# A decoder trunk on one core: both norms' sides by tiles of 128 tokens, and five weight slots with the low part over the raw weights

## The reference, cut to what matters

```python
for l in range(2):
    x = layer_norm(ALPHA * x + 0.5 * swiglu(x, ffn1_w_gate[l], ffn1_w_up[l], ffn1_w_down[l]), ...)
    x = layer_norm(ALPHA * x + hybrid_mixer(x, ...), ...)
    x = layer_norm(ALPHA * x + 0.5 * swiglu(x, ffn2_w_gate[l], ffn2_w_up[l], ffn2_w_down[l]), ...)

def swiglu(x, w_gate, w_up, w_down):              # inner width 2816
    return (silu(x @ w_gate) * (x @ w_up)) @ w_down
```

## Time and profile before

| | |
|---|---|
| median of 3 runs | 1401.45 us (1401.25 to 1403.24) |
| the profiled execution | 1403.12 us, its span 1400.8 us |
| PE busy | 97% of the span |
| DVE, ACT, POOL busy | 66%, 47%, 5% |
| mean granted clock of PE | 0.992 |
| HBM read | 232 MB, 167 GB/s over the span |

### The profile page before, as it was taken

One profiled execution on the slowest core, in us unless ns is written; L12 is line 12 of the kernel. 1 busy time (PEld: TensorE's weight loads), 2 busy tenths in 40 slices (PEclk: granted clock), 3 DMA queues, 4 the chain that ended last, 5 costly groups with the idle time before them and its releaser, 6 DMA issues.

```text
span 1400.8 us, 20707 instructions
## 1 busy us (share of the span) xinstructions
PE 1353.8 (97%) x8440; PEld 1203.2 (86%) x8440; DVE 928.8 (66%) x978; ACT 663.4 (47%) x674; POOL 69.9 (5%) x59
## 2 busy tenths in 40 slices
PE   7999989999999999999999999899999999999997
PEld 6888879899899978888878888798998999788886
DVE  5665666788885656565665666676988656666565
ACT  5444455574354354444454444555744543544442
POOL 2980000000000000000000000000000000000000
PEclk9999999999999999999999999999999999999999
DMA  8655644544355545655545565436434555365562
GB/s 275 227 180 180 192 151 133 164 136 123 121 154 185 174 150 183 195 191 180 172 158 180 185 195 190 143 122 185 121 99 142 178 184 173 110 227 180 180 191 79
DMA packets 182312, 234.19 MB, mean 167 GB/s; under 512 B 5808, under 2 KB 161072, under 8 KB 182128
## 3 DMA queue, kind: packets, MB, share of 16 engines
q1 hardware_dynamic: 182016, 231.68, 52.1%
q0 software_dynamic: 240, 1.71, 0.4%
HBM read 232.33 MB, written 1.05 MB: 167 GB/s over the span
## 4 chain that ended last, share of the span: by engine, by line
PE 95%; DVE 3%; ACT 2%; issue 0%; DMA 0%; SPq 0%; DVEq 0%; ACTq 0%
PE ps L1283 24%; PE ps L1294 21%; PE ps L1223 11%; PE ps L1224 11%; PE ps L1225 11%; PE ps L1282 10%; PE ps L1286 1%; DVE wlo L748 1%; PE ps L1243 1%; PE ps L1392 1%; DVE z L864 1%; ACT whi L463 1%; PE ps L1410 0%; PE ps L1430 0%; PE ps L1440 0%; PE ps L1435 0%
## 5 line engine op out<-in xcount | busy, mean ns | idle before, releaser
L748 DVE TENSOR_TENSOR wlo<-raw,whi 128x2048 fp32r<-128x2048 f32 (+2 forms) x221 | 497.6, 2253 | 188.6 <-ACT whi L463 188.5
L463 ACT ACTIVATE whi<-raw 128x2048 fp32r<-128x2048 f32 (+2 forms) x221 | 415.3, 1881 | 354.2 <-PE ps L1225 206.2
L1283 PE MATMUL ps<-xpair,whi 128*128 128x512 f32 x1408 | 489.5, 397 | 5.0 <-DVE xpair L805 5.0
L1282 PE MATMUL ps<-xpair,wlo 128*128 128x256 f32 x1232 | 345.5, 280 | 0.0
L1283 PEld LDWEIGHTS ps<-xpair,whi 128*128 128x128 f32 x1408 | 255.2, 188 | 54.5 <-DVE xpair L805 5.7
L1223 PE MATMUL ps<-xpair,whi 128*128 128x256 f32 (+2 forms) x896 | 259.7, 290 | 10.7 <-DVE xpair L805 5.4
L1224 PE MATMUL ps<-xpair,whi 128*128 128x256 f32 (+2 forms) x896 | 255.9, 286 | 0.0
L1225 PE MATMUL ps<-xpair,wlo 128*128 128x256 f32 (+2 forms) x896 | 255.8, 286 | 0.0
L1282 PEld LDWEIGHTS ps<-xpair,wlo 128*128 128x128 f32 x1232 | 233.1, 189 | 8.1
L1223 PEld LDWEIGHTS ps<-xpair,whi 128*128 128x128 f32 (+2 forms) x896 | 170.4, 190 | 13.4 <-issue 12.4
L1224 PEld LDWEIGHTS ps<-xpair,whi 128*128 128x128 f32 (+2 forms) x896 | 170.3, 190 | 2.0 <-issue 1.0
(11 more groups left out here) (221 smaller groups left out, 1680.2 us busy)
## 6 DMA issues: line engine op xcount, KB each, us to landing
raw<-w_in SPq DMA_DIRECT2D x60, 1024.0 KB, 5.2
raw<-ffn_w_up SPq DMA_DIRECT2D x44, 1024.0 KB, 5.3
raw<-ffn_w_down SPq DMA_DIRECT2D x44, 1024.0 KB, 4.9
raw<-ffn_w_gate SPq DMA_DIRECT2D x43, 1024.0 KB, 5.4
raw<-w_br SPq DMA_DIRECT2D x12, 1024.0 KB, 5.0
raw<-w_out SPq DMA_DIRECT2D x8, 1024.0 KB, 4.9
raw<-mla_w_uq SPq DMA_DIRECT2D x4, 576.0 KB, 3.9
raw<-mla_w_ukv SPq DMA_DIRECT2D x2, 1024.0 KB, 5.6
```

What stands on the lines that cost most here:

```text
L463: act.activation(whi[:, k % RING, 0:n], raw[:, k % RING, 0:n], ACT.Copy).then_inc(w_hi, 1)
L748: dve.tensor_tensor(wlo[:, k % RING, 0:n], raw[:, k % RING, 0:n], whi[:, k % RING, 0:n].bitcast(F32), ALU.subtract).then_inc(w_lo, 1)
L1282: pe.matmul(ps[:, bank + c, 0:SEQ], wl[:, kk, cols], xhi[:, kk, :], start=False, stop=False)
L1283: last = pe.matmul(ps[:, bank + c, :], wh[:, kk, cols], xpair[:, kk, :, :], start=kk == 0, stop=kk == KC - 1)
```

## The change

Tokens cross every norm in two tiles of 128. In the last two units of a stage (`last_rows`) PE does banks 0 and 1 of both, then the rest; the transposes of tile 0 stand between products of bank 2. DVE and ACT share a tile's rows (lower 512 features on DVE, upper on ACT), and DVE orders its work tile by tile. The next stage begins with work that a single tile allows: in an FFN the gate and up unit of step 0 are done with the tokens as stationary operand (`tile_gate`, `tile_up`), and the product is transposed (`tile_split`); in a mixer mv comes first, by halves of the depth with 512 columns. `RING` is five, `wlo` lies over `raw`, `load` waits for `w_used` of the unit five before, and `hi` waits for the load alone; `hi` and `lo` of the next stage's first units stand in the last FFN step. The loops over the FFN's steps are written out. The last up unit is done in three terms without a sum on ACT and DVE. On ACT the silu of `ml_qk` goes behind the copies of `k_nope`; the gate units use banks 5 and 6 and the branches 7 and 4. `g_row` and `b_row` lie in another region.

```diff
-RING = 3
+RING = 5
-    raw = sb("raw", [P, RING, UNIT])
-    whi, wlo = sb("whi", [P, RING, UNIT], F32R), sb("wlo", [P, RING, UNIT], F32R)
+    r_raw = region(4 * RING * UNIT)
+    raw, wlo = place("raw", [P, RING, UNIT], F32, r_raw), place("wlo", [P, RING, UNIT], F32R, r_raw)
+    whi = sb("whi", [P, RING, UNIT], F32R)
...
+    BANK |= {"mv0": 6, "mv1": 7}
+    GATE_BANK, BRANCH_BANK = (5, 6), (7, 4)
+    FFN_GATE, FFN_UP, TILE_BANK = 6, 4, (6, 4)
...
-            sp.wait_ge(w_lo, free_no(l, k, f))
+            if n >= RING:
+                sp.wait_ge(w_used, done_no(n - RING))
...
+                load_x(1)
...
     @block.scalar
-            act.wait_ge(w_loaded[k % RING], loaded_no(l, k, f))
-            act.wait_ge(w_used, free_no(l, k, f))
+            act.wait_ge(w_loaded[n % RING], (n // RING + 1) * 16)
...
+            if nth:
+                hi(base + 2)
+            tile_silu(0)
+            hi(base + 3)
+            tile_silu(1)
+            hi(base + 4)
+            for j in range(1, NF):
+                hi(base + 3 * j + 2)
+                gate_of(j)
+                silu_of(j)
+                if base + 3 * j + 3 < N_UNITS:
+                    hi(base + 3 * j + 3)
+                if j < NF - 1:
+                    up_of(j)
+                if base + 3 * j + 4 < N_UNITS:
+                    hi(base + 3 * j + 4)
...
+        def layer_norm(l, w):
+            turn = l * 3 + w
             act.activation(warm[:, :], C("eps", 1), ACT.Sqrt)
+            for t in range(TT):
+                act.wait_ge(ln_var, tile_no(turn, t))
+                act.activation(std[:, t:t + 1], mv[:, t, 1:2], ACT.Sqrt,
                                bias=C("eps", 1, 1)).then_inc(ln_std, 1)
...
+                act.wait_ge(ln_shift, tile_no(turn, t))
+                act.activation(z[:, t, 512:], ps[:, 2 * t + 1, :], ACT.Identity, bias=shift[:, t:t + 1],
+                               scale=rstd[:, t:t + 1]).then_inc(rows_up, 1)
+                scale_x(turn + 1, t)
...
-            hi(l, m0 + 11)
-            act.wait_ge(conv_tap, l * 32 + 16)
-            act.activation(ml_qk[:, 0:4, :], ml_qk[:, 0:4, :], ACT.Silu).then_inc(qk_silu, 1)
+            hi(m0 + 13)
             act.wait_ge(k_done, l + 1)
             copy(flat(k_nope[:, 0:2, :]), "kn0").then_inc(k_copied, 1)
             copy(flat(k_nope[:, 2:4, :]), "kn1").then_inc(k_copied, 1)
...
+            hi(m0 + 14)
+            act.wait_ge(conv_tap, l * 32 + 16)
+            act.activation(ml_qk[:, 0:4, :], ml_qk[:, 0:4, :], ACT.Silu).then_inc(qk_silu, 1)
...
+        scale_x(0, 0)
         act.wait_ge(half_loaded, 16)
         act.activation(whi[:, 0, 0:UNIT // 2], raw[:, 0, 0:UNIT // 2], ACT.Copy).then_inc(half_hi, 1)
         act.wait_ge(w_loaded[0], 16)
         act.activation(whi[:, 0, UNIT // 2:], raw[:, 0, UNIT // 2:], ACT.Copy).then_inc(w_hi, 1)
+        scale_x(0, 1)
+        hi(1)
+        hi(2)
...
     @block.vector
+            for j in range(1, NF):
+                lo(base + 3 * j + 2)
+                if j == 1:
+                    tile_split()
+                gate_sum(j)
+                if base + 3 * j + 3 < N_UNITS:
+                    lo(base + 3 * j + 3)
+                product(j)
+                split(j)
+                if base + 3 * j + 4 < N_UNITS:
+                    lo(base + 3 * j + 4)
...
+        def scale_x(stage, t):
+            dve.wait_ge(rows_turned, half_no(stage, t, 0))
...
+                for k in range(4):
+                    last = dve.tensor_scalar(xf[:, k, tok], ps[:, 4, k * P:(k + 1) * P], par_col(l, "ln_g", 8 * w + k),
+                                             par_col(l, "ln_b", 8 * w + k), ALU.mult, ALU.add)
+            last.then_inc(x_lower, 1)
+            dve.wait_ge(x_lower, tile_no(stage, t))
+            split_x(stage, t, 0)
...
             measure(0)
             measure(1)
             aggregate(0)
-            measure(2)
             invert(0)
             if last_turn:
                 store_rows(0)
+                measure(2)
                 measure(3)
...
+            normalise(0)
+            scale_x(turn + 1, 0)
+            measure(2)
+            dve.wait_ge(x_upper, tile_no(turn + 1, 0))
+            split_x(turn + 1, 0, 1)
             measure(3)
             aggregate(1)
             invert(1)
...
+            normalise(1)
+            scale_x(turn + 1, 1)
+            dve.wait_ge(x_upper, tile_no(turn + 1, 1))
+            split_x(turn + 1, 1, 1)
...
     @block.tensor
+        def last_rows(n, pick, stage):
+            for bank in range(4):
+                for kk in range(2):
+                    if bank == 2 and kk == 0:
+                        tile_rows(n - 1, 1, pick[0]).then_inc(w_used, 1)
+                    last = tokens(n, bank, kk, *pick[1](kk, bank // 2), False, True)
+                    if kk == 1 and bank < 3:
+                        last.then_inc(y_bank, 1)
+                    if bank == 2 and kk == 0 and stage < 3 * DEPTH:
+                        turn_rows(stage, 0)
+            last.then_inc(w_used, 1)
...
+            tile_gate(0)
+            turn_rows(stage, 1)
+            if stage:
+                tile_up(0)
+            tile_gate(1)
+            if stage == 0:
+                tile_up(0)
+            tile_up(1)
...
+                if j == 1:
+                    pe.wait_ge(tok_hid, tile_no(nth, 1))
+                    for c in range(2):
+                        for t in range(TT):
+                            last = pe.transpose(ps[:, FFN_UP + 1, c * SEQ + t * P:c * SEQ + (t + 1) * P],
+                                                hid[:, t * SEQ + c * P:t * SEQ + (c + 1) * P], ident)
+                    last.then_inc(hid_turned, 1)
+                    paired(FFN_UP, up)
+                    pe.wait_ge(hid_lo, step_no(l, w, 0))
+                    paired(FFN_UP + 1, up).then_inc(w_used, 1)
...
+            first_values(0, 0)
+            turn_rows(stage, 1)
+            first_values(0, 1)
+            first_values(1, 0).then_inc(w_used, 1)
+            first_values(1, 1).then_inc(w_used, 1)
+
+            project(2, "c0")
...
-            pe.wait_ge(k_copied, l * 2 + 2)
-            half_tokens(10, ("mv0", "mv1"), 0)
-            half_tokens(11, ("mv0", "mv1"), 256)
...
                         if b == h == 0:
-                            pe.wait_ge(rg_ready, l * 2 + 2)
-                        two_chunks(4 + i, k).then_inc(w_used, 1)
+                            pe.wait_ge(mo_ready, l * 2 + i + 1)
+                        two_chunks(GATE_BANK[i], k).then_inc(w_used, 1)
```

More of the change, by code:

```diff
@@ L39 @@
 MIX_BASE = U_FFN
[L40 removed]
+N_UNITS = DEPTH * U_LAYER
 C_MQ, C_MV, C_GATES, C_MO = 704, 1728, 2240, 2248
@@ new lines, in scale_x @@
+        def scale_x(stage, t):
+            act.wait_ge(rows_turned, half_no(stage, t, 1))
+            tok = slice(t * P, (t + 1) * P)
+            for k in range(4, KC):
+                src = ps[:, 5, (k - 4) * P:(k - 3) * P]
+                if stage == 0:
+                    last = act.activation(xf[:, k, tok], src, ACT.Copy)
+                else:
+                    l, w = (stage - 1) // 3, (stage - 1) % 3
+                    last = act.activation(xf[:, k, tok], src, ACT.Identity, bias=par_col(l, "ln_b", 8 * w + k),
+                                          scale=par_col(l, "ln_g", 8 * w + k))
+            last.then_inc(x_upper, 1)
@@ L808, in layer_norm @@
-        def layer_norm(l, w, early):
+            if nth:
+                lo(base + 2)
+            tile_product(0)
+            lo(base + 3)
+            tile_product(1)
+            lo(base + 4)
+            for j in range(1, NF):
+                lo(base + 3 * j + 2)
[8 more added lines that the diff above has]
+                    lo(base + 3 * j + 4)
@@ new lines, in split_x, with scale_x @@
+        def split_x(stage, t, half):
+            part, tok = slice(4 * half, 4 * half + 4), slice(t * P, (t + 1) * P)
+            dve.tensor_copy(xhi[:, part, tok], xf[:, part, tok]).then_inc(x_hi, 1)
+            dve.wait_ge(x_hi, half_no(stage, t, half))
+            dve.tensor_tensor(xlo[:, part, tok], xf[:, part, tok], xhi[:, part, tok].bitcast(F32),
+                              ALU.subtract).then_inc(x_ready, 1)
+        def scale_x(stage, t):
+            dve.wait_ge(rows_turned, half_no(stage, t, 0))
+            tok = slice(t * P, (t + 1) * P)
+            if stage == 0:
+                last = dve.tensor_copy(xf[:, 0:4, tok], ps[:, 4, :].rearrange("p (k n) -> p k n", k=4))
+            else:
+                l, w = (stage - 1) // 3, (stage - 1) % 3
+                for k in range(4):
[4 more added lines that the diff above has]
+            split_x(stage, t, 0)
@@ new lines, in two_chunks, with tile_columns, paired @@
+                last = features(ps[:, bank, c * SEQ:(c + 1) * SEQ], n, width, slice(c * P, (c + 1) * P), xh, xl, n_k)
+            return last
+        def tile_columns(out, n, kk, x_kk, t, start, stop):
+            wh, wl = slot(n, out.shape[1])
```

(39 more changed lines are left out.)

798 lines of the change are left out of this document (380 added, 418 removed).

## The result

The changed kernel takes 1363.44 us (median; 1362.52 to 1364.15) against 1402.35 us of the kernel before on the same chip: ratio 0.9715, interval 0.9701 to 0.9728. The forecast was 1366.2 us with a range of 1359 to 1382. The profiled execution took 1363.81 us with a span of 1361.5, so 39.3 us of span went where 35.3 had been forecast.

A forecast was written before the change was run, and what follows sets the result against it. TensorE (PE), busy 97% of the 1400.8 us span, was taken to bound the kernel. The terms summed to -35.3 us, taking the 1401.45 us median to a forecast of 1366.2 us, range 1359 to 1382.

The forecast's parts named there:

- five crossings: At the five norm crossings, working tile by tile leaves 3.0 us lost in place of 27.2: -24.2 us.
- last wait of an FFN: At four FFN ends, the wait for the last unit's `lo` shrinks by 0.3 us each: -1.2 us.
- k_nope and rot_sw: In the mixers, PE's wait for k_nope goes and 0.6 us for rot_sw stays: -2.8 x 2 = -5.6 us.
- rg with its drop: In the mixers, gates on free banks end the rg wait and its clock drop: -4.2 x 2 = -8.4 us.
- products and switches: PE's work: mv and rv -1.4, tile products +1.9, transposes of hid +1.75, switches +2; sum +4.3 us.
- start: At the kernel's start, units 0 and 1 end at 29.2 us against 27.3: +1.9 us (0 to 3.5).
- Rival 1: At crossings, tile chains on DVE stay on the path and the clock drops: 18 us more, 1384; chance 0.12.
- Rival 4: At crossings, the tile order brings nothing, tile 1 ends each as before: +21 us, 1387; chance 0.03.
- rival 2: At crossings, transposes and wait count as one idle, so only the clock drops: 8 us more, 1374; chance 0.10.
- Rival 3: In the mixer, rotation, conv or softmax chain come 2.5 us late in four places: +10 us, 1376; chance 0.10.
- Rival 5: In FFN steps, `lo` in place is slow; at 5.5 us for one, +116 us, 1482; chance 0.03.
- Rival 6: Better than forecast: no switching cost on PE, clock up earlier at the start: -4 to -7 us, 1361; chance 0.09.

The follow-up runs named there:

- Experiment 1: Changed kernel with the last two units of each stage in plain order, tile 0's transposes behind all of it: 1377.15 us, ratio 0.9814.
- experiment 6: Changed kernel with three more 512-column statistics operations on DVE in tile 1's chain at five crossings: 1364.99 us, ratio 0.9731.
- experiment 2: Changed kernel with ACT's first silu of ml_qk ahead of the k_nope copies again: 1370.31 us, ratio 0.9768.
- experiment 4: Kernel before with only the mixer's waits mended (gates wait for the bank, silu behind the k_nope copies), three slots and old norm kept: 1388.99 us, ratio 0.9900.
- experiment 3: Changed kernel whose first two gate units wait for both rg copies again, on their new banks: 1365.23 us, ratio 0.9733.
- Experiment 5: Changed kernel with four slots instead of five (RING = 4), nothing else: 1403.21 us, ratio 1.0004.
- Experiment 8: Changed kernel with an unused tile ahead of mv: 1359.02 us (ratio 0.9680) with 32 bytes a partition, 1363.57 us (0.9713) with 64.
- Experiment 9: Changed kernel with start and DVE order at mixer crossings rearranged (1361.95 us), plus 96 unused bytes ahead of mv: 1355.63 us, ratio 0.9657.

## Why the prediction was right, and where it was off

The waits went where the forecast had them go; where it was off, sizes were. One cause, that of the rg wait, was told too simply. In the trace the difference of the two spans divides like this (us, forecast and measured; gaps and blocks of products from start to start):

| term | forecast | measured |
|---|---|---|
| five crossings | -24.2 | -22.9 (27.2, the prediction's figure, to gaps of 4.3) |
| last wait of an FFN, four times | -1.2 | -0.8 (gone; it was a gap of 0.2) |
| k_nope and rot_sw | -5.6 | -5.8 |
| rg with its drop | -8.4 | -8.7 (96 products of rg and gate in 15.9, now 11.6) |
| products and switches | +4.3 | +0.7 (the rest of the sum) |
| start | +1.9 | +0.3 |
| end | -2.05 | -2.1 |
| sum | -35.3 | -39.3 |

*The crossings.* Most of the chain's times came within 0.1 us, one did not: the lower half of x was ready 0.3 us late (U+9.5 for 9.2). The scalings, which no row of before showed, took 1.37 for the four instead of 1.15 (0.34 each, inside the bounds of 0.2 and 0.47). PE asked 0.2 early, as the switches between products and transposes cost nothing there (36 products and 8 transposes in 9.28 us), so a gap of 0.35 us that was not forecast stands at each mixer entry. That tile 1's rows still came at U+13.4 for 13.5 has some luck in it: their part of the chain took 4.0 us and not 4.3. They were waited for as forecast: gaps of 1.05 us at the two mixer entries (forecast 1.2) and 0.5 at the FFN entries (forecast 0.2). Experiment 1 shows the order's share and experiment 6 that tile 1's chain sets the time there. Rivals 1 and 4 fell with these rows.

*The clock.* There is no drop behind the start, so rival 2 did not come true; that it could not have is not shown. At a mixer's entry 8 transposes and a wait stand together for 1.9 us, at 1.00. In experiment 6 the wait is 2.2 us with 0.87 us of transposes behind it, 3.1 together, and the clock stays at both mixer entries. In experiment 1 the transposes are ahead of a wait of 2.3 us, and it falls at the first of these places and not at the other; it also falls at two of the three FFN entries, where 12 transposes and waits of 1.0 and 0.6 us lie between two products. In experiment 2 a wait of 2.3 us with no transposes by it brought a fall once in two. The Trainium skill's rule ("TensorE: Matmul & The Clock Gate", Part 4: PE-mode transpose) would make one idle of each stretch of transposes and waits. The falls at the FFN entries of experiment 1 fit it, as no single wait there is longer than 1.0 us. Experiment 6 shows no such fall, but doesn't refute it, since of the stretches of 3.3 us in experiment 1 some brought a fall and some didn't. So the forecast of no drop was right for the stretches of 1.9 us that the kernel has, and nothing here says how near it is.

*The mixer.* The sizes were right (-14.5 for -14.0, and 14.0 in experiment 4). Of rg I named one cause, the free banks; there are two, the banks and the weight copy that no longer waits ahead of rg on ACT, and either nearly does it (experiments 3 and 4). The size held because it took the whole gap once. Rival 3 fell: nothing in the mixer got late.

*The last FFN step.* Forecast with 0.25 us to spare; `hlo_last` is ready at 192.84, 0.45 before the last unit starts, and no wait stands there. Experiment 5 shows how thin it is: with one slot less PE waits 3.1 us there.

*PE's work*, the term missed by most. I priced the products of mv and rv, tokens stationary and 512 columns, by the down unit's 0.233 us; they ran at 0.227, so these eight units save 2.5 us and not 1.4. The 2 us for switches between transposes and products is the other term that was too large, as the last two units of the first FFN show none of it. Over the whole kernel products and switches can't be told apart (a nanosecond in the median pace of the 2128 products of 256 columns with `wlo` is 2 us), so the rest of the 3.6 us stays unassigned. Experiments 8 and 9 suggest why the price for mv and rv was too high: the down products, by which I priced, change their pace by some 5 ns with the place of a tile, and with the hidden pairs moved by 96 bytes they too run at 227.

*The start.* I had the first half of the weights' low part done at 11.0 on DVE; it was done at 9.8, PE's stream began at 9.86 and the clock rose at 15.3 us, 1.2 earlier than before. So units 0 and 1 end at 27.6 us for a forecast 29.2. The step that failed is the landing, taken from the copy at 9.65 and moved by 1 us only; in the kernel before that half had landed at 8.6, and its copy stood behind a copy of x on ACT until 9.65. Now it starts at 7.47.

*The end.* The last statistics start at 1354.82, PE's last product at 1354.39: 0.43, as forecast.

```profile
1354.39 0.40 PE L1373 MATMUL ps<-whi,hlo_last 128*128 128x512 f32 x1
1354.82 0.70 DVE L889 BATCH_NORM_STATS2 stats<-ps 128x6 f32<-128x512 f32 x1 [0.70 <-PE ps L1373]
```

Rival 5, the slow subtraction in place, fell with its first row. Rival 6 described the outcome best: little switching cost and the clock up early, at 1363.4 between the forecast and its 1361.

## What to carry to other kernels

Where a reduction over a whole tile blocks the bound engine, reorder the last two units so that one tile is finished early, and count what cover each tile's chain has; here its steps could be forecast within 0.3 us from the durations of single operations. Buffers that look like plenty in the steady loop are set by the places where the order of units changes: one slot less cost the whole gain. And before an experiment is read, look whether the code around it kept its pace: a few added bytes hid 5 of 6.5 us.
